# Streaming the expert weights of a mixture-of-experts block two matrix rows at a time: w_up in 2 MB transfers, w_down in 8 KB runs, and the feature order changed to match

## The reference, cut to what matters

```python
h = rms_norm(x, norm_ffn_g)                       # (512, 1024)
logits = h @ w_router + b_router                  # 32 experts
top_logit, top_e = lax.top_k(logits, 4)           # 4 experts for each token
gate = softmax(top_logit)
# for each expert e and each token x of it:
u = x @ w_up[e] + b_up[e]                         # w_up[e]: 1024 x 2048 (8 MB)
glu = minimum(u[:, :1024], 7.0); lin = clip(u[:, 1024:], -7.0, 7.0)
act = glu * sigmoid(1.702 * glu) * (lin + 1.0)
y = act @ w_down[e] + b_down[e]                   # w_down[e]: 1024 x 1024 (4 MB)
# the output adds gate * y over a token's 4 experts; a last rms_norm follows
```

## Time and profile before

| | |
|---|---|
| median of three timed runs | 1719.64 us (1718.55 to 1720.01) |
| profiled execution, its own time | 1717.27 us |
| span of the profiled execution | 1715.5 us |
| PE busy | 1632.3 us, 95% |
| DVE busy | 552.4 us, 32% |
| DMA | 467.53 MB, mean 273 GB/s over the span |

### The profile page before, as it was taken

How to read it: one execution, slowest core, us unless ns; L and a number is a source line. 1 busy time by engine, 2 the same in 40 slices (tenths; PEclk the granted TensorE clock), 3 DMA queues, 4 the chain that set the end, 5 groups by cost and what they waited for, 6 DMA issues and landing times.

```text
span 1715.5 us, 31426 instructions
## 1 busy us (share of the span) xinstructions
PE 1632.3 (95%) x12231; PEld 744.1 (43%) x12232; DVE 552.4 (32%) x1444; ACT 256.7 (15%) x558; POOL 212.5 (12%) x202
## 2 busy tenths in 40 slices
PE   7998799999998689999999999999999999999993
PEld 3443356545545234444444444444434444444442
DVE  3223445331223332233223322242224222422241
ACT  3022233311211001011101110011101110111012
POOL 1000000060010101211121112111211121111111
PEclk9999899999998789999999999999999999999997
DMA  6211022051112779999999999999999999999994
GB/s 223 98 49 49 1 101 96 1 190 49 50 49 98 290 281 381 368 373 390 376 375 377 386 378 376 373 393 384 369 370 400 380 375 374 386 394 369 382 386 159
DMA packets 105620, 467.53 MB, mean 273 GB/s; under 512 B 14158, under 2 KB 14210, under 8 KB 72720
## 3 DMA queue, kind: packets, MB, share of 16 engines
q1 hardware_dynamic: 91768, 441.58, 65.6%
q0 software_dynamic: 13744, 25.46, 6.3%
q10 hardware_dynamic: 72, 0.02, 0.0%
HBM read 456.91 MB, written 18.87 MB: 277 GB/s over the span
## 4 chain that ended last, share of the span: by engine, by line
PE 93%; DVE 3%; issue 1%; DMA 1%; ACT 1%; POOL 0%; ACTq 0%; POOLq 0%; DVEq 0%
PE bank L892 39%; PE bank L670 23%; PE bank L920 13%; PE bank L929 6%; PE bank L881 1%; PE bank L860 1%; PE bank L870 1%; PE bank L817 1%; PE bank L800 1%; DVE arena L1322 1%; PE bank L862 1%; PE bank L873 1%; PE bank L907 1%; PE bank L688 1%; PE bank L744 1%
## 5 line engine op out<-in xcount | busy, mean ns | idle before, releaser
L892 PE MATMUL bank<-ring,arena 128*32 128x512 f32 x6144 | 681.5, 596 | 0.7 <-ACT arena L1132 0.7
L892 PEld LDWEIGHTS bank<-ring,arena 128*32 128x32 f32 x6144 | 228.2, 110 | 404.7 <-issue 336.7
L920 PE MATMUL bank<-ring,arena 128*32 128x512 f32 x2048 | 267.8, 592 | 0.0
L670 PE MATMUL bank<-ring,actT 128*128 128x512 f32 x448 | 202.6, 609 | 0.1
L1497 DVE TENSOR_SCALAR tokA<-bank 64x512 f32<-64x512 f32 x64 | 43.7, 683 | 419.7 <-PE bank L892 418.7
L929 PE MATMUL bank<-ring,arena 128*32 128x512 f32 x1024 | 157.9, 592 | 0.0
L920 PEld LDWEIGHTS bank<-ring,arena 128*32 128x32 f32 x2048 | 112.8, 110 | 96.3
L576 POOL DMA_INDIRECT arena<-h_rows,arena x33 | 35.1, 1064 | 903.2 <-DVE arena L1481 902.9
L670 PEld LDWEIGHTS bank<-ring,actT 128*128 128x128 f32 x448 | 86.2, 197 | 101.2 <-issue 100.5
L1137 ACT ACTIVATE tokA<-tokA 128x512 f32<-128x512 f32 x32 | 20.2, 630 | 505.5 <-DVE tokA L1497 505.5
L670 PE MATMUL bank<-actT,ring 128*128 128x512 f32 x192 | 83.5, 593 | 0.0
(11 more groups left out here) (286 smaller groups left out, 1336.5 us busy)
## 6 DMA issues: line engine op xcount, KB each, us to landing
ring<-in_w_up SPq DMA_DIRECT2D x256, 1024.0 KB, 6.9
ring<-in_w_down SPq DMA_DIRECT2D x128, 1024.0 KB, 8.2
ring<-in_w_in SPq DMA_DIRECT2D x12, 1024.0 KB, 7.5
ring<-in_w_ck SPq DMA_DIRECT2D x4, 1024.0 KB, 6.3
ring<-in_w_out SPq DMA_DIRECT2D x4, 1024.0 KB, 6.3
ring<-in_w_cv SPq DMA_DIRECT2D x4, 1024.0 KB, 7.9
ring<-in_w_cq SPq DMA_DIRECT2D x4, 1024.0 KB, 6.7
ring<-in_w_co SPq DMA_DIRECT2D x4, 1024.0 KB, 6.2
```

The costliest lines, as they stand in the source:

```text
L670: mm = pe.matmul(o, lhsT, rhs, start=(k == 0), stop=(k == KT - 1))
L892: mm = pe.matmul(bank[g][32 * t:32 * t + 32, :], lhsT, w[:, 512 * t:512 * t + 512], start=False, stop=(k == KT - 1))
L920: mm = pe.matmul(bank[3][r:r + 32, :], hTA[:, k % 4, g, k // 4, :], w[:, 512 * t:512 * t + 512], start=False, stop=(k == KT - 1))
```

## The change

Three things change together. (1) A load of `w_up` is 2 MB: 256 matrix rows, two neighbouring rows (16 KB in one piece) on each partition, into two neighbouring slots. SyncE waits until both slots are free, and one semaphore (of the first slot) tells that both are filled; TensorE waits once for a pair. (2) A load of `w_down` stays 1 MB, but a partition's two rows are neighbours, 8 KB in one piece. (3) Partition p of chunk pair c now holds features 256c + 2p and 256c + 2p + 1 where it held 256c + p and 256c + 128 + p. So the columns of the normalized tokens and of the activations are written in the order that pairs up the same features: L1209 becomes two instructions of 512 columns that read every second column, and L1509 and L1516 write alternately to two places 128 columns (512 bytes) apart. The router's weights are loaded in the same order.

```diff
         def up_chunk(e, c):
-            return A["w_up"][0][e, P * c:P * c + P, :]
+            return A["w_up"][0].rearrange("e (c p u) n -> e c p (u n)", p=P, u=2)[e, c // 2, :, :]
 
         def down_chunk(e, c):
-            return A["w_down"][0].rearrange("e (k p) n -> e p k n", p=P)[e, :, 2 * c:2 * c + 2, :]
+            return A["w_down"][0].rearrange("e (c p u) n -> e c p (u n)", p=P, u=2)[e, c, :, :]
 
         slot_dense = [16 * len(range(s, DENSE, RING)) for s in range(RING)]
-        def expert_chunk_in(eng, q, o):
-            eng.wait_ge(chunk_in[o % RING], q * (16 * PER_SLOT) + (slot_dense[o % RING] + 16 * (o // RING + 1)))
+        one_up = [("up", k) for k in range(UP_CHUNKS)]
+        one_down = [("down", k) for k in range(DOWN_CHUNKS)]
+        stream = one_up + (one_up + one_down) * (NE - 1) + one_down + (one_up + one_down) * MO
+        signals = [c for c, (kind, k) in enumerate(stream) if kind == "down" or k % 2 == 0]
+
+        def signalled(c):
+            return slot_dense[c % RING] + 16 * len([d for d in signals if d <= c and d % RING == c % RING])
+
+        def expert_chunk_in(eng, q, o, q0):
+            if isinstance(q, int):
+                eng.wait_ge(chunk_in[o % RING], signalled(q * PER_EXPERT + o))
+            else:
+                first = signalled(q0 * PER_EXPERT + o)
+                each = signalled((q0 + 1) * PER_EXPERT + o) - first
+                eng.wait_ge(chunk_in[o % RING], q * each + (first - q0 * each))
...
             def load_up(q, o, e):
-                for c in range(UP_CHUNKS):
-                    sp_.wait_ge(chunk_used, q * PER_EXPERT + (o + c + 1))
+                for c in range(0, UP_CHUNKS, 2):
+                    sp_.wait_ge(chunk_used, q * PER_EXPERT + (o + c + 2))
                     slot = (o + c) % RING
-                    sp_.dma_start(ring_flat[:, slot, :], up_chunk(e, c)).then_inc(chunk_in[slot], 16)
+                    sp_.dma_start(ring_flat[:, slot:slot + 2, :].rearrange("p s n -> p (s n)"),
+                                  up_chunk(e, c)).then_inc(chunk_in[slot], 16)
...
             def up_pair(q, o, pair):
+                expert_chunk_in(pe, q, o + 2 * pair, 0 if o else NE)
                 for k in (2 * pair, 2 * pair + 1):
-                    expert_chunk_in(pe, q, o + k)
...
-                        ins = v.scalar_tensor_tensor(out=h_tok[:, b, :], in0=x_res[:, b, :], scalar=rstd[:, b:b + 1],
-                                                     in1=gffn, op0=ALU.mult, op1=ALU.mult)
+                        for u in range(2):
+                            ins = v.scalar_tensor_tensor(out=h_tok[:, b, :].rearrange("p (c u n) -> p c u n", n=P, u=2)[:, :, u, :],
+                                                         in0=x_res[:, b, :].rearrange("p (c n u) -> p c n u", n=P, u=2)[:, :, :, u],
+                                                         scalar=rstd[:, b:b + 1],
+                                                         in1=gffn.rearrange("p (c n u) -> p c n u", n=P, u=2)[:, :, :, u],
+                                                         op0=ALU.mult, op1=ALU.mult)
...
+            def in_pairs(t):
+                return t.rearrange("p (c n u) -> p c n u", n=P, u=2)
+
+            def by_pairs(t):
+                return t.rearrange("p (c u n) -> p c n u", n=P, u=2)
...
-                v.tensor_tensor(actA, linA, sigA, ALU.mult).then_inc(actA_ready, 1)
+                v.tensor_tensor(by_pairs(actA), in_pairs(linA), in_pairs(sigA), ALU.mult).then_inc(actA_ready, 1)
...
-                v.tensor_tensor(actB[0:64, :], linB[0:64, :], sigB[0:64, :], ALU.mult).then_inc(actB_ready, 1)
+                v.tensor_tensor(by_pairs(actB[0:64, :]), in_pairs(linB[0:64, :]), in_pairs(sigB[0:64, :]), ALU.mult).then_inc(actB_ready, 1)
```

More of the change, by code:

```diff
@@ L1 @@
+import itertools
 import math
@@ L466, in load_down @@
                     slot = (o + c) % RING
-                    sp_.dma_start(ring_flat[:, slot, :].rearrange("p (k n) -> p k n", k=2), down_chunk(e, c)).then_inc(chunk_in[slot], 16)
+                    sp_.dma_start(ring_flat[:, slot, :], down_chunk(e, c)).then_inc(chunk_in[slot], 16)
             load_up(0, 0, 0)
@@ L539, in _ @@
             g.wait_ge(mixed_ready, NB)
-            g.dma_start(w_rt[:, :, :], A["w_router"][0].rearrange("(k p) n -> p k n", p=P)).then_inc(router_in, 16)
+            g.dma_start(w_rt.rearrange("p (c u) n -> p c u n", u=2), A["w_router"][0].rearrange("(c p u) n -> p c u n", p=P, u=2)).then_inc(router_in, 16)
             for q in range(3):
@@ L912, in down @@
                 for c in range(DOWN_CHUNKS):
-                    expert_chunk_in(pe, q, o + c)
+                    expert_chunk_in(pe, q, o + c, 0 if o == 2 * UP_CHUNKS else NE)
                     for u in range(2):
```

## The result

The changed kernel takes 1721.32 us (median of 20 runs), the kernel before 1718.68 us (20 runs beside them). The ratio is 1.0016, with a 95% interval of 1.0009 to 1.0022: 2.7 us slower (1.5 to 3.8), less than what I had called no change (3.4 us). The forecast was 3.0 us (1722.6). The times of either kernel fall into two groups, four short ones (1713.60 to 1714.67 us before, 1716.99 to 1717.85 after) and sixteen longer ones (1716.71 to 1720.01, 1719.76 to 1723.45), and the changed kernel is slower in both.

The account below looks back on a forecast made before the run. The prediction took the loop to be bound by TensorE, with DMA just inside it. Stores 2.0 + first products 1.0 + 31 rounds 0 = +3.0 us on the median 1719.64 gave 1722.6 us, range 1719.0 to 1728.0 (8 in 10).

Parts of the forecast that it names:

- The loop is bound by TensorE: Expert loop: TensorE never waits for a DMA, the DMA queues run just inside it, and rounds stay 34.46 us apart.
- Turns between the queues: Ahead of the experts: stores alternate packet by packet with 16 KB prefetch pieces and end later, +2.0 us (0.1 to 2.5).
- the clock adds about 1 us to either side: After TensorE's waits: half clock for a while, so more waiting can bring full level back earlier or later, about 1 us.
- First products: First expert: strided writes of L1509 and L1516 lengthen the chain TensorE waits for, +1.0 us (0 to 1.4).
- The split of L1209: Last block ahead of the experts: two instructions instead of one, with strided reads, +0.1 to +1.1 us.
- Loop, 0: 31 rounds: w_up pairs land after 7.6 to 9.6 us of the 11.4 available, so no stall, 0 us.
- rival (a): Loop: its reserve is used up, a late pair costs up to 1.9 us; put at 1729 us, slower, chance 0.14.
- w_down loads: Loop: they keep their size and 13 us, and 8 KB pieces instead of 4 KB can only shorten them, 0.
- The gathers in the loop: Beside 16 KB loads: at worst 3.9 us longer against 3.6 us of reserve, median leaves 2.3 us; 0 us.
- The signs: Expected profile: 2 MB landings 7.6 to 9.6 us, last store near 14, first transposes about 574, wait for L1489 near 8.9.
- Rival (c): DMA queues: 16 KB pieces travel as 8 KB packets, stores lose only 0.1 to 1.1 us; 1721.2 us, same, chance 0.17.
- Rival (d): Before the experts: prefetch and stores finish sooner, gather 1 us earlier, half-level stretch shrinks, returning 3 us; 1715.6, faster, chance 0.06.

Follow-up runs that it names:

- Experiment 1: The kernel before, with w_up in 2 MB transfers of 8 KB pieces in the old row order; w_down and VectorE as before: 1717.41 us, ratio 0.9994.
- experiment 2: The changed kernel's feature order, VectorE strides and 8 KB w_down pieces, but w_up in 1 MB transfers of 8 KB pieces: 1718.44 us, ratio 0.9993 to the kernel before.
- experiment 4: The changed kernel, with the second and third 2 MB prefetch transfers waiting until the stores have landed: 1721.77 us, ratio 1.0014 to the kernel before.
- experiment 7: The kernel before, with two more useless 512-column VectorE products ahead of the last one of the first expert: 1719.16 us, ratio 1.0012.
- experiment 8: The kernel before, with the acc_rows wait and the final norm weights' load moved behind the first gather, which waits for h_rows alone: 1714.38 us, ratio 0.9978.

## Why the prediction was right or wrong

The sign, the size (3.0 against 2.7 us) and the places were right; two of the terms were not what they seemed.

- **The loop is bound by TensorE.** Right: of the 29 rounds behind the restart's, 27 take 34.47 us as before.
- **Turns between the queues, +2.0.** Right as far as the gather: one packet for one, +2.0 us on the store (12.4 to 14.4), +2.05 on the gather. Experiment 1 ties it to the 16 KB piece, experiment 2 shows it gone with pieces of 8 KB, experiment 4 shows the loads to be nearly all of the delay. That the 2.0 came out exactly is partly luck. My sum took the end of the stores from 8.2 to 10.2 us after 557. The last store of before landed at 565.9, which is 8.9 after 557, and that of after at 568.0 once aligned, which is 11.0; read rightly, my 10.2 would have given +1.3. What failed is that I carried the 2.0 to the end. The gather landed 0.35 us sooner, with all six megabytes of loads in (at 569.24, 1.6 us before it went out; before, the last of them came 0.9 us behind the gather's start), and 0.9 us came back because the half-level stretch did not move with TensorE's start. The prediction had "the clock adds about 1 us to either side" and did not ask on which side.
- **First products, +1.0.** The mechanism is right, the size is not: 0.36 us each instead of 0.51, and 0.55 on the path. The casts by which I priced them gave 1.0 ns per element, the products 0.7 (0.36 us over 512). The rule of the Trainium skill that I had set beside it, "Vector Engine (DVE) Microarchitecture Reference", § 5.2 (0.7 us together), came closer for the writes. For the reads it did not hold: it prices a hopping source like a hopping destination, and here two passes with stepping reads cost 0.1 us (its table has no step of two words). For them the 16-byte line of the Trainium skill, "SBUF — State Buffer", § Door 1: The DMA port swizzle, did.
- **The split of L1209, +0.1 to +1.1, within the stores' term.** Right, at 0.1.
- **The missing term.** The round behind the restart grew by 0.96 us. That and the 0.9 given back nearly cancel, so the total hides two errors of the same kind, a clock whose half-level stretch ends where it ends. The 2.9 us of the profile are 2.05 (gather) - 0.35 (its landing) - 0.91 (clock) + 0.55 (products) + 0.96 (clock) + 0.49 (late pairs) + 0.1 behind the loop.
- **Loop, 0.** The step "no stall" failed, by 0.5 us. The 11.4 us that a pair has and the worst landing (10.7 to 13.3) were right; I took the median for the answer, though among some 120 pairs one or two late ones are enough. Such longer rounds occur in the profiles of all five kernels with pairs and all the products (34.59 to 35.66 us), and in none of the four with 1 MB loads (before, experiments 2, 7 and 8); that makes it the pairing's, at 0.2 to 1.2 us a run. It is rival (a) in small.
- **w_down loads, "can only shorten".** Wrong: 8.3 to 10.2 us, though in larger pieces. They share the engines with 2 MB transfers that are issued in one go. In experiment 2, without pairs, they land after 8.5; in experiment 1, with pairs but w_down in its old 4 KB pieces, after 10.5. So it is the pairing. The 13 us of reserve hid it.
- **The gathers in the loop.** 5.8 to 7.2 us in the median, 8.2 at most: well inside the 3.6 us that I had left, as forecast.
- **The signs.** Landing of the pairs 9.6 us (7.6 to 9.6 forecast); the store near 14 us: 14.4; first transposes +2 us: 575.28, which is 3.25 us later, or 1.7 aligned; the wait for L1489 near 8.9: 8.5.
- **Rival (c)**, 16 KB travelling as 8 KB packets, is out: the loads moved 2.80 MB in 187 packets. **Rival (d)** did not come from the change. Its mechanism exists all the same: experiment 8 sends the gather out 0.37 us earlier, the half-level stretch shrinks by 3.4 us, and the median falls by 3.8 us.

What stays open is where the half-level stretches end. No kernel was profiled twice. The 0.9 us given back and the 0.96 us lost are those of one execution each and need not be what the stretches cost in every one; that they are what separates the short and the long executions of one kernel is likely, but not shown.

## What to carry to other kernels

Larger DMA pieces are not free where another queue holds something that is waited for: the DMA engines took turns by packet here (316 to 277, 187 to 153), so doubling a piece took share from what stood beside it, and together with the pairing it bought nothing, even where DMA was the bound (405 and 403 GB/s). Look at what the critical wait really needs: taking one store that the gather does not read out of that wait brought more than any piece size, mainly by making every execution as short as the short ones of before. And with a TensorE that restarts at half clock, add up a delay only as far as the next restart; behind it, measure.

## What was not expected of the hardware

- Granted clock: 2.05 us of later work came to +1.70, +0.79, +1.34, +2.30 us at the next four points, since TensorE's half-level stretch (27.3 us long in both kernels) did not wait for the work. A half-level stretch costs 0.5 us per us of matmuls in it.
- The same 2.05 us ended as +2.91 us with products of 1.05 us at the restart and as +0.29 us with products of 0.69 (one profiled execution each; 0.5 and 0.2 us of it are late pairs).
- VectorE, float32 from SBUF: stepping by two on the reads, 0.71 us per 512 columns, is nearly as fast as adjacent (0.69); stepping by 128 on the write is 1.05. In the loop, beside loads, the stepping reads rise to 0.75, adjacent ones don't.
- Under a saturated load, 8 KB pieces for w_down instead of 4 KB brought 8.3 to 8.5 us, not less (experiment 2).
